# Three X units take both parts of h in one wide product, a VectorE pass joins the halves, and three small steps change place

## The reference

```
h = rms_norm(x, mix_norm_g);  xr, yg, q, k, v = split(h @ w_in)
xr = causal_depthwise_conv(xr, lru_conv_w, lru_conv_b)          # 4 taps
y_lru = rg_lru(xr, w_a, b_a, w_i, b_i, lam) * gelu(yg)
y_attn = attention(rms_norm(q), rms_norm(k), v)                 # 8 heads, one block
x = x + concat(rms_norm(y_lru), rms_norm(y_attn)) @ w_out
hf = rms_norm(x, ffn_norm_g)
up = causal_depthwise_conv(hf @ w_up, ffn_conv_w, ffn_conv_b)   # 3 taps
x = x + (gelu(gate) * val) @ w_down
```

## Time and profile before

| | |
|---|---|
| median of 3 runs | 289.14 us (288.96 to 289.18) |
| profiled execution | 288.88 us |
| its span, first to last instruction | 287.2 us |
| PE busy | 282.8 us (98%) |
| DVE busy | 243.8 us (85%) |
| ACT busy | 202.7 us (71%) |
| granted PE clock | 1.000 over the span |

### The profile page before, as it was taken

One profiled execution on the slowest core, in us unless ns is written; L12 is line 12 of the kernel. 1 busy time (PEld: TensorE's weight loads), 2 busy tenths in 40 slices (PEclk: granted clock), 3 DMA queues, 4 the chain that ended last, 5 costly groups with the idle time before them and its releaser, 6 DMA issues.

```text
span 287.2 us, 4943 instructions
## 1 busy us (share of the span) xinstructions
PE 282.8 (98%) x1610; PEld 244.5 (85%) x1610; DVE 243.8 (85%) x452; ACT 202.7 (71%) x394; POOL 11.1 (4%) x26
## 2 busy tenths in 40 slices
PE   7999999999999999999999999999999999999996
PEld 7688998788788999888888888888888888888885
DVE  2998898999999888999887788878887888887775
ACT  4883599999997687777567656665776566567640
POOL 3000005500000000000000000000000000000000
PEclk9999999999999999999999999999999999999999
DMA  7999950434074705375737455444636534300004
GB/s 276 428 421 419 412 186 0 148 110 183 6 268 168 280 16 186 118 283 175 275 143 289 148 173 231 165 175 148 276 146 211 227 146 165 129 0 0 2 0 146
DMA packets 8256, 52.25 MB, mean 182 GB/s; under 512 B 944, under 2 KB 1328, under 8 KB 2224
## 3 DMA queue, kind: packets, MB, share of 16 engines
q1 hardware_dynamic: 8064, 51.50, 47.8%
q0 software_dynamic: 176, 0.53, 0.5%
HBM read 50.98 MB, written 1.05 MB: 181 GB/s over the span
## 4 chain that ended last, share of the span: by engine, by line
PE 97%; DMA 1%; DVE 1%; ACT 0%; issue 0%
PE bank L1470 25%; PE bank L1479 13%; PE bank L1082 13%; PE bank L1083 13%; PE bank L1086 13%; PE bank L1142 3%; PE bank L1261 3%; PE bank L1422 3%; PE bank L1433 1%; PE bank L1265 1%; DMA x_tok<-in_x_dram 1%; PE bank L1210 1%; PE bank L1368 1%; PE bank L1345 1%; PE bank L1241 1%; PE bank L1186 1%
## 5 line engine op out<-in xcount | busy, mean ns | idle before, releaser
L713 DVE TENSOR_TENSOR w_lo<-raw,w_hi 128x1024 fp32r<-128x1024 f32 x93 | 111.1, 1222 | 9.8 <-ACT w_hi L386 9.3
L386 ACT ACTIVATE w_hi<-raw 128x1024 fp32r<-128x1024 f32 x85 | 86.3, 1058 | 0.3
L1470 PE MATMUL bank<-h_both,w_hi 128*128 128x512 f32 x320 | 76.0, 389 | 0.0
L1470 PEld LDWEIGHTS bank<-h_both,w_hi 128*128 128x128 f32 x320 | 59.9, 188 | 12.4
L1479 PEld LDWEIGHTS bank<-h_both,w_lo 128*128 128x128 f32 x320 | 41.2, 191 | 1.6
L1479 PE MATMUL bank<-h_both,w_lo 128*128 128x256 f32 x320 | 41.7, 283 | 0.0
L624 ACT ACTIVATE tanh_a<-bank 128x256 f32<-128x256 f32 x44 | 16.5, 377 | 34.6 <-PE bank L1479 34.6
L632 ACT ACTIVATE xc<-ygate,par 128x256 f32<-128x256 f32 x44 | 26.5, 601 | 15.5 <-DVE ygate L1005 15.5
L1083 PE MATMUL bank<-w_lo,act_hi 128*128 128x512 f32 (+1 forms) x90 | 34.8, 387 | 0.0
L1082 PE MATMUL bank<-w_hi,act_hi 128*128 128x512 f32 (+1 forms) x90 | 34.8, 387 | 0.0
L1086 PE MATMUL bank<-w_hi,act_lo 128*128 128x512 f32 (+1 forms) x90 | 34.6, 384 | 0.0
(11 more groups left out here) (205 smaller groups left out, 411.8 us busy)
## 6 DMA issues: line engine op xcount, KB each, us to landing
raw<-in_stream_dram SPq DMA_DIRECT2D x47, 1024.0 KB, 4.8
out_dram<-x_tok SPq DMA_DIRECT2D x3, 256.0 KB, 2.1
x_tok<-in_x_dram SPq DMA_DIRECT2D x1, 512.0 KB, 3.3
x_tok<-in_x_dram SPq DMA_DIRECT2D x2, 256.0 KB, 5.9
p_T<-in_gates_dram POOLq DMA_DIRECT2D x1, 512.0 KB, 9.5
out_dram<-x_tok SPq DMA_DIRECT2D x2, 128.0 KB, 2.0
par<-in_params_dram SPq DMA_DIRECT2D x1, 117.0 KB, 5.8
mix_g<-in_params_dram POOLq DMA_DIRECT2D x1, 4.0 KB, 5.5
```

What stands on the lines that cost most here:

```text
L386: act.activation(hi_tile(u)[:, :], raw_unit(u), ACT.Copy).then_inc(hi_done, 1)
L713: dve.tensor_tensor(w_lo[u % RING][:, :], raw_unit(u), hi_tile(u)[:, :].bitcast(F32), ALU.subtract).then_inc(lo_done, 1)
L1470: pe.matmul(acc[:, :], whi[:, kc, :], h_both[:, kc, :, :].rearrange("p b t -> p (b t)"), start=kc == 0, stop=False)
```

## The change

Three of the four X units (`SIDES = 3`) are computed as the Y units are: one product of 512 columns and one of 256 per chunk in place of three of 256. The body of `y_unit` becomes `sides_unit`, which both call. A new `x_join(c)` on DVE adds the two halves of `X_ACC[c]` into `decay[:, c, :]`, an SBUF tile that is free at that time, and the convolution of those three reads from there. The fourth X unit stays as it was. In ACT's order `conv_first(1)` moves behind the copies of q and k, `conv_first(2)` behind `exps(0)`, `conv_first(3)` behind `exps(1)`. In DVE's order the splits of units 13 and 14 move back, and `conv_rest(3)` moves ahead of both `row_reciprocals`. The split of unit 27 goes between the second and the third `y_add`.

```
+SIDES = 3
+        x_lru = [decay[:, c, :] if c < SIDES else bank[4 + c][:, 0:SEQ] for c in range(LC)]
...
             def conv_first(c):
-                act.wait_ge(unit_used, U_X + c + 1)
+                if c < SIDES:
+                    act.wait_ge(x_joined, c + 1)
+                else:
+                    act.wait_ge(unit_used, U_X + c + 1)
...
             his(12, 13)
             conv_first(0)
-            conv_first(1)
...                     # q and k copied out
+            conv_first(1)
             his(14)
             act.activation(lam_z, ..., ACT.Abs)
-            conv_first(2)
             act.activation(lam_u, ..., ACT.Exp, scale=-1.0)
             exps(0)
+            conv_first(2)
             exps(1)
+            conv_first(3)
             exps(2)
-            conv_first(3)
             exps(3)
...
+            def x_join(c):
+                dve.wait_ge(unit_used, U_X + c + 1)
+                dve.tensor_reduce(x_lru[c], X_ACC[c][:, :].rearrange("p (b t) -> p t b", b=2), AX_X,
+                                  ALU.add).then_inc(x_joined, 1)
...
-            los(12, 13)
+            x_join(0)
+            los(12)
+            x_join(1)
             conv_rest(0)
+            los(13)
             conv_rest(1)
-            los(14)
             shift(0)
+            x_join(2)
             shift(1)
             shift(2)
             shift(3)
             conv_rest(2)
+            conv_rest(3)
             row_reciprocals(0)
-            conv_rest(3)
             row_reciprocals(2)
             y_join(0)
-            los(15, 16)
+            los(14, 15, 16)
...
-            for i in range(len(Y_PIECES)):
-                y_add(i)
-            los(27, U_FFN)
+            y_add(0)
+            y_add(1)
+            los(27)
+            y_add(2)
+            y_add(3)
+            los(U_FFN)
...
+            def sides_unit(u, acc):
...                     # the body that y_unit had
-            cols_unit(U_X, X_ACC[0][:, 0:SEQ])
-            cols_unit(U_X + 1, X_ACC[1][:, 0:SEQ])
+            sides_unit(U_X, X_ACC[0])
+            sides_unit(U_X + 1, X_ACC[1])
             pe.wait_ge(qk_norm, 2 * TT)
             for c in range(LC):
                 transpose_qk(c)
-            cols_unit(U_X + 2, X_ACC[2][:, 0:SEQ])
+            sides_unit(U_X + 2, X_ACC[2])
```

More of the change, by code:

```diff
@@ L210, in build_layer @@
         lru_in, scan_done = sem("lru_in"), sem("scan_done")
-        y_joined = sem("y_joined")
+        y_joined, x_joined = sem("y_joined"), sem("x_joined")
         ygate_done, y_done, y_sq_done, y_chunks = sem("ygate_done"), sem("y_done"), sem("y_sq_done"), sem("y_chunks")
@@ L466, in conv_first @@
             def conv_first(c):
-                act.wait_ge(unit_used, U_X + c + 1)
+                if c < SIDES:
+                    act.wait_ge(x_joined, c + 1)
+                else:
+                    act.wait_ge(unit_used, U_X + c + 1)
                 w3 = CONV_W + (LRU_CONV - 1) * LC + c
-                act.activation(xc[:, c, :], X_ACC[c][:, 0:SEQ], ACT.Identity, bias=par[:, CONV_B + c:CONV_B + c + 1],
+                act.activation(xc[:, c, :], x_lru[c], ACT.Identity, bias=par[:, CONV_B + c:CONV_B + c + 1],
                                scale=par[:, w3:w3 + 1]).then_inc(conv_base, 1)
@@ L799, in conv_rest @@
                     col = CONV_W + (LRU_CONV - 1 - back) * LC + c
-                    tap = dve.scalar_tensor_tensor(xc[:, c, back:SEQ], X_ACC[c][:, 0:SEQ - back],
+                    tap = dve.scalar_tensor_tensor(xc[:, c, back:SEQ], x_lru[c][:, 0:SEQ - back],
                                                    par[:, col:col + 1], xc[:, c, back:SEQ], ALU.mult, ALU.add)
@@ L1252, in gates_product @@
                 ins.then_inc(gates_done, 1)
[L1254 to L1258, removed]
+            def sides_unit(u, acc):
+                whi, wlo = by_chunk(w_hi[u % RING]), by_chunk(w_lo[u % RING])
                 pe.wait_ge(hi_done, hi_count(u))
@@ L1266, in y_unit @@
                 ins.then_inc(unit_used, 1)
+            def y_unit(c):
+                if c >= 2:
+                    pe.wait_ge(y_joined, c - 1)
+                sides_unit(U_Y + c, Y_SIDES[c % 2])
             pe.wait_ge(hi_done, hi_count(U_K))
```

## The result

The changed kernel takes 289.56 us (median of 21 runs, 289.37 to 289.74), the kernel before 289.10 in the same comparison (21 runs, 288.96 to 289.47). The ratio is 1.0015, with a 95% interval of 1.0009 to 1.0021: slower by 0.15%, clear of the timing's noise. The profiled execution took 289.46 us with a span of 287.7, 0.58 above the one before.

The account below looks back on a forecast made before the run. PE was taken as the bound (97% of the span): -0.32 X units, +0.35 score_pair(6), +0.05 attend, +0.27 transpose_f(1), +0.05 POOL = +0.40; profiled 288.88 becomes 289.28, median 0.26 above, 289.5. Range 288.85 to 290.0.

Parts of the forecast that it names:

- each of its three places: PE's predicted waits: score_pair(6) and attend for ACT, +0.35 and +0.05; transpose_f(1) at the norm, +0.27 from DVE's lateness.
- PE's gain: X units: 24 wide products save 0.013 each, 0.32 us in all; other bound 0.27, from 0.09 a unit.
- The estimate of 0.06: X units on PE: by the skill's rule for isolated products, 24 products fewer save 0.06 us.
- DVE's order up to `y_join(0)`: DVE from 35.66: joins, splits and taps in sequence, y_join(0) at 48.42 instead of 48.74; DVE 0.81 late afterwards.
- No new wait of PE between 45 and 53: Sign in the next profile: any PE wait between 45 and 53 would mean a wait had been missed.
- POOL beside DVE: Three splits, not two, beside POOL's scaling: extra DVE cost between nothing and two times 0.18, taken as 0.05.
- POOL and DVE in each other's way: Rival, 17%: all splits and small lambda steps slowed, DVE 1.1 to 1.6 late, 289.8 to 290.2; decides from 1.04.
- The room ahead of `transpose_f(1)`: Norm: PE late by DVE's lateness less 0.46, not under 0.08; 0.27 absorbed at f_add(0), 0.16 at first f_part.
- ACT: conv_first(3) waits for X3 until 45.62, leaving ACT 0.52 late: 47.84 instead of 47.32, nothing to catch up on.
- Unit 27's move: Split ahead of two y_adds: ready some 1.4 sooner, closes a PE hole of 0.3 or 0.6, costs nothing.
- an exclusive port: Rival, 2%: each of three splits waits behind a POOL instruction of 0.91; lateness rises 2.6, loss about 3, 292.
- One sign: Next profile, near 103.4: PE idle ahead of line 1389 by some 0.2 to 0.5.

Follow-up runs that it names:

- i_after_late29: Changed kernel with unit 28's split moved from ahead of f_add(0) to unit 29's place, unit 29's behind the last f_part: 289.44 us, ratio 1.0013.
- l_all: Changed kernel with lo(14) ahead of y_join(0), conv_first(3) behind exps(2), row_reciprocals(0) ahead of conv_rest(3), splits of units 28 and 29 later: 288.99 us, ratio 0.9995.
- b_after_lo27_back: Changed kernel with unit 27's split put back behind all four y_adds: 290.00 us, ratio 1.0028.
- c_before_lo27_join: Kernel before, with unit 27's split moved and one extra unused join on DVE ahead of y_join(0), X units as before: 289.32 us, ratio 1.0004.
- d_after_join: Changed kernel with one extra unused join on DVE ahead of y_join(0): 290.29 us, ratio 1.0036.
- g_base3_late: Changed kernel with conv_first(3) back behind exps(2) on ACT: 289.59 us, ratio 1.0015.

## Why the prediction was right

The forecast was 289.5, +0.40; measured 289.56, +0.46. Its mechanism held at each of its three places, and the two sizes that decided the total were off in opposite directions.

- **PE's gain**: 0.32 taken, 0.27 measured, the other bound given. The three units took 2.77, 2.80 and 2.80, Y0 2.79. The estimate of 0.06 that the prediction set beside it is out: the trace decides.
- **DVE's order up to `y_join(0)`**: 48.42 forecast, 48.63 less the 0.17 of the late start is 48.46. No new wait of PE between 45 and 53.
- **POOL beside DVE**: mis-sized. 0.05 was taken, within bounds of nothing and 0.36; the runs show 0.30, and where it arose was wrong too. The splits were not it: from 49.24 to the lambda chain at 52.75 three took 3.51, 0.12 over three times 1.13, where in the kernel before two had lost 0.20 by the same count. It was the chain (+0.77 ahead of it, +1.07 behind), and in it one step that met the start of a POOL instruction. With 1.06 DVE passed the threshold of 1.04 of the case "POOL and DVE in each other's way", short of its 1.1 to 1.6 and with one of its two causes in small: no split was slowed more than before, one lambda step was. By the prediction's own room of 0.46 that would have cost 0.60. The prediction also set POOL's 1.66 beside a median of 0.91 that mixes two shapes; the instruction was a 128x128 one, and those take 0.60 undisturbed.
- **The room ahead of `transpose_f(1)`**: mis-sized. 0.46 was counted (0.27 at `f_add(0)`, 0.16 at the first `f_part`, and a rest of 0.03 at the load); the runs show 0.60. The term left out is `f_add(4)`, which had waited 0.13 for PE in the kernel before; the first `f_part` is at +0.61 on DVE and `f_add(4)` at +0.48. So 1.06 - 0.60 = 0.46 stands where 0.86 - 0.46 = 0.40 was forecast. DVE 0.20 later than forecast, the room 0.14 larger: that the total came within 0.06 is in part luck, as these two errors cancelled. So is the 0.25 of the one lambda step, which hangs on how two engines happened to meet.
- **ACT**: +0.52 forecast, +0.58 measured. The difference is PE's smaller gain: `conv_first(3)` waits for X3 and started at 45.85 - 0.17 = 45.68 instead of 45.62. The base passes that read SBUF took 0.60, 0.65 and 0.59, against 0.54 to 0.57 from PSUM; I had taken nothing for this, and it cost nothing, since all three stand ahead of the 0.31 that ACT idled for X3. The Trainium skill ("VectorE: DVE Perf Modes", The TRN2 errata) gives ScalarE 52 cycles more for a source in SBUF than for one in PSUM, by the page's 1.2 GHz an estimate of 0.04 us; the trace agrees for two of the three, and the third took 0.09 more than from PSUM. At `attend` PE was at +0.22 instead of +0.08: ACT's 0.07, and 0.11 instead of 0.04 between the end of `v_out(0)` and the load.
- **Unit 27's move**: said to close a hole of 0.3 to 0.6; taken back, it costs 0.44 in the median and 0.42 at `transpose_f(1)`.
- **The rest**: no stall in the feed-forward part, no wait of PE, ACT or DVE for a transfer between 30 and 120 us, and nothing was seen of an exclusive port at the splits in the size of that rival. One sign came out otherwise: PE was to idle 0.2 to 0.5 ahead of line 1389, but the loss at the norm is in two parts, 0.09 at the first feed-forward products and 0.12 ahead of `transpose_f(1)`, and the load shows an idle time of 0.08.

What isn't settled: where the 0.35 ahead of `f_add(0)` in `i_after_late29` and `l_all` comes from, and whether `l_all` is truly faster than the kernel before. Its position at the end says 0.16, its interval allows from 0.14% faster to 0.03% slower.

## What to carry to other kernels

When one engine is the bound by a hair, list for each of its waits how long the condition has already held, and take off what the change adds to the other engine's lateness: here 0.5, 0.5 and 0.07 us of slack stood against 0.58 more on ACT, twice, and 1.06 on DVE (some 0.6 of which was taken up by waits on the way), and PE's 0.27 could not get past them. Count an engine's lateness from the last place where it idled: in the changed kernel the 0.60 of an added instruction was paid in full behind `y_join(0)` though DVE is idle for 15% of the span. And before work is added to such an engine, use up its idle time first: putting one displaced split ahead of a wait instead of behind it gave back half of the loss.

## What the runs showed of the hardware

What a short DVE instruction loses to POOL depends on how the two meet. In the changed kernel one of DVE's steps on 128x4 elements took 0.41 us instead of 0.17, and the spacing to the next was 0.45 instead of 0.20. It began 0.08 behind the start of a POOL instruction that scales a 128x256 tile in SBUF. The chain's other steps ran beside POOL too and took 0.16 to 0.26, as in the kernel before (but for L882's 0.43, which cost nothing). Six of the thirteen traces have a step like it, not always the same one: `b_after_lo27_back`, `i_after_late29`, `c_before_lo27_join`, `d_after_join`, `g_base3_late` and the change itself. In each it began 0.07 or 0.08 behind the start of a POOL instruction and took 0.41. Steps that began 0.15 or 0.16 behind such a start took 0.22 or 0.23, and those that began with it or up to 0.05 behind lost at most 0.03.

POOL loses more than DVE: beside DVE's three splits its 128x128 instruction took 2.21 instead of 0.60 in the changed kernel, while no DVE split beside it took more than 1.50 instead of 1.22 (`c_before_lo27_join`). The Trainium skill ("SBUF — State Buffer", Who interferes with whom) has it that DVE with two SBUF inputs and a POOL instruction that reads SBUF contend, and that the one that issues first holds the shared port while the other blocks fully. The traces agree that both sides lose at times. They don't show the full block: the step at 55.73 lost 0.24, while the POOL instruction ahead of it had 0.84 still to run.
